# First block's query and key norm: mean squares with tokens on partitions, and one root and one reciprocal for all eight pairs

## What is computed

```python
h = rmsnorm(x, norm1_g[l])
proj = h @ w_in[l]
u, v_a, q, k, v_b = jnp.split(proj, splits, axis=-1)
...
q = rmsnorm(q.reshape(bsz, s, B_HEADS, 2, B_HEAD_DIM), q_norm_g[l]).transpose(0, 2, 3, 1, 4)
k = rmsnorm(k.reshape(bsz, s, B_HEADS, 2, B_HEAD_DIM), k_norm_g[l]).transpose(0, 2, 3, 1, 4)
```

## Time and profile before

| | us |
|---|---|
| median of 3 runs | 2310.82 |
| lowest and highest | 2306.65, 2314.41 |
| the profiled execution | 2307.06 |
| its span in the profile | 2305.3 |

### The profile page before, as it was taken

The page is one execution under the profiler, slowest core; times in us unless marked ns, Lnnn a source line. Parts: engine busy times, 40 slices in busy tenths (PEclk is TensorE's granted clock), DMA queues, the critical chain, the costliest instruction groups (busy, mean ns, idle before and its releaser), DMA issues.

```text
span 2305.3 us, 32023 instructions
## 1 busy us (share of the span) xinstructions
PE 2232.5 (97%) x13582; PEld 1820.1 (79%) x13582; DVE 1315.1 (57%) x1860; ACT 700.0 (30%) x966; POOL 206.1 (9%) x233
## 2 busy tenths in 40 slices
PE   7989988999999999999999999999999999999998
PEld 6778984555478888889679888888888888968998
DVE  5677544333377557543557755745756633656554
ACT  5445331111142122123453211223312212454333
POOL 2100200000011000030021100003000002002000
PEclk9999999999999999999999999999999999999999
DMA  9753756999956456432114545624636423405573
GB/s 296 250 207 116 250 206 250 420 421 421 404 172 192 136 156 184 124 116 69 49 38 128 173 144 166 184 89 122 183 117 202 147 86 106 128 20 144 160 203 117
DMA packets 377548, 408.86 MB, mean 177 GB/s; under 512 B 11625, under 2 KB 342878, under 8 KB 361150
## 3 DMA queue, kind: packets, MB, share of 16 engines
q1 hardware_dynamic: 355886, 325.55, 42.9%
q0 software_dynamic: 20928, 80.14, 10.5%
q10 hardware_dynamic: 592, 1.12, 0.1%
HBM read 405.71 MB, written 1.05 MB: 176 GB/s over the span
## 4 chain that ended last, share of the span: by engine, by line
PE 88%; DVE 7%; ACT 2%; DMA 1%; issue 1%; SPq 0%; POOL 0%; DVEq 0%; ACTq 0%
PE B L1815 23%; PE B L1817 22%; PE B L1816 22%; PE B L2210 6%; PE B L2230 3%; PE B L2181 2%; PE B L2169 2%; DVE LO L680 1%; PE B L2536 1%; DVE R L691 1%; DVE HF L1061 1%; PE B L2510 1%; ACT HI L1378 1%; PE B L1948 1%; PE B L2520 1%
## 5 line engine op out<-in xcount | busy, mean ns | idle before, releaser
L1815 PE MATMUL B<-hH,HI 128*128 128x512 f32 (+1 forms) x1936 | 661.6, 342 | 14.0 <-DVE hL L1049 6.5
L1816 PE MATMUL B<-hL,HI 128*128 128x512 f32 (+1 forms) x1936 | 653.5, 338 | 0.0
L1817 PE MATMUL B<-hH,LO 128*128 128x512 f32 (+1 forms) x1936 | 653.2, 337 | 0.0
L680 DVE TENSOR_TENSOR LO<-RAW,HI 128x2048 fp32r<-128x2048 f32 (+3 forms) x218 | 443.6, 2037 | 115.6 <-ACT HI L1378 109.8
L1378 ACT ACTIVATE HI<-RAW 128x2048 fp32r<-128x2048 f32 (+3 forms) x218 | 368.6, 1692 | 347.4 <-PE B L1817 274.0
L1815 PEld LDWEIGHTS B<-hH,HI 128*128 128x128 f32 x1936 | 368.2, 190 | 65.3 <-DVE LO L680 12.6
L1817 PEld LDWEIGHTS B<-hH,LO 128*128 128x128 f32 x1936 | 368.3, 190 | 39.7
L1816 PEld LDWEIGHTS B<-hL,HI 128*128 128x128 f32 x1936 | 368.6, 190 | 37.5 <-issue 0.2
L1815 PE MATMUL B<-aH,HI 128*128 128x512 f32 (+1 forms) x770 | 269.3, 350 | 0.4 <-DVE LO L680 0.4
L1817 PE MATMUL B<-aH,LO 128*128 128x512 f32 (+1 forms) x770 | 269.0, 349 | 0.0
L1816 PE MATMUL B<-aL,HI 128*128 128x512 f32 (+1 forms) x770 | 268.2, 348 | 0.0
(11 more groups left out here) (377 smaller groups left out, 2649.4 us busy)
## 6 DMA issues: line engine op xcount, KB each, us to landing
RAW<-in_ffn_w_gu SPq DMA_DIRECT2D x176, 512.0 KB, 5.2
W<-in_w SPq DMA_DIRECT2D x78, 1024.0 KB, 11.9
MADW<-in_ada_w POOLq DMA_DIRECT2D x112, 512.0 KB, 3.7
W2T<-in_w SPq DMA_DIRECT2D x39, 1024.0 KB, 12.1
RAW<-in_w_in SPq DMA_DIRECT2D x60, 512.0 KB, 5.1
RAW<-in_ffn_w_down SPq DMA_DIRECT2D x56, 384.0 KB, 3.7
RAW<-in_ffn_w_down SPq DMA_DIRECT2D x56, 320.0 KB, 4.3
RAW<-in_w_out SPq DMA_DIRECT2D x24, 512.0 KB, 4.4
```

Source lines behind the costliest of these rows:

```text
L680: V.tensor_tensor(LO[s][:, :words], RAW[s][:, :words], HI[t.hi[s]][:, :words].bitcast(F32), ALU.subtract).then_inc(lo_done[s], 1)
L1815: mm(o, wh, xh, start=first, stop=False, **more)
L1816: mm(o, wh, xl, start=False, stop=False, **more)
L1817: return mm(o, wl, xh, start=False, stop=last, **more)
```

## The change

For each pair, the four blocks of 128 features by 128 tokens of `SQ` now become the stationary operand, and two columns of `MEAN_HD` the moving one. The means come out with tokens on partitions, two columns for each block: 64 columns in B[2] for all eight pairs. After chunk 8, ACT takes one root of 128 x 64 and DVE one reciprocal of 128 x 64. PE then spreads the scales back to features with 64 products of a repeated column (64 columns wide) and the identity, four pairs after chunk 9 and four after chunk 10. DVE multiplies each pair with its gain and the scales straight from PSUM, four pairs in its step 10 and four in its step 11.

```diff
@@ names @@
+        FIRST_HEADS = (0, 4, 1, 5, 2, 6, 3, 7)
+        FIRST_BANKS = (0, 1, 3, 2)
+        FIRST_SCALES = 2 * TB * HEADS * 2
@@ VectorE @@
+            def scaled(n):
+
+                c = FIRST_HEADS[n]
+                got("spread_done")
+                gain = GQ[:, 0:1] if c < 4 else PT[:, KN:KN + 1]
+                V.scalar_tensor_tensor(pair(QK, c), pair(QK, c), gain, B[FIRST_BANKS[n % 4]][:], ALU.mult, ALU.mult)\
+                    .then_inc(E["qk_ready"], 1)
+
             for c in range(12):
                 prep()
                 t.use()
-                if 1 <= c <= 8:
-                    r = R[(c - 1) % 2][:]
-                    rstd(r)
-                    gain = GQ[:, 0:1] if c - 1 < 4 else PT[:, KN:KN + 1]
-                    V.scalar_tensor_tensor(pair(QK, c - 1), pair(QK, c - 1), gain, r, ALU.mult, ALU.mult)\
-                        .then_inc(E["qk_ready"], 1)
+                if c == 8:
+                    got("std_ready")
+                    r = R[0][:, 0:FIRST_SCALES]
+                    V.reciprocal(r, r).then_inc(E["qr_ready"], 1)
+                if c >= 9:
+                    for n in ((), range(0, 4), range(4, 8))[c - 9]:
+                        scaled(n)
@@ ScalarE @@
                     A.activation(pair(QK, c), B[4 + c % 2][:], ACT.Copy)
+                    if c >= 2:
+                        got("stats_done")
                     A.activation(SQ[c % 2][:], B[4 + c % 2][:], ACT.Square).then_inc(E["sq_ready"], 1)
...
-                if 1 <= c <= 8:
-                    if c >= 3:
-                        act.wait_ge(E["qk_ready"], c - 2)
-                    root(B[2 + (c - 1) % 2][:], R[(c - 1) % 2][:])
+                if c == 8:
+                    got("stats_done")
+                    root(B[2][:, 0:FIRST_SCALES], R[0][:, 0:FIRST_SCALES])
@@ TensorE @@
-            def stats(m, i, b, n=512):
-
-                claim(b, "std_ready")
-                got("sq_ready")
-                mm(B[b][:, :n], mat(m), SQ[i % 2][:, :n], start=True, stop=True).then_inc(E["stats_done"], 1)
-
+            def first_squares(i):
+
+                if i == 0:
+                    claim(2, "std_ready")
+                got("sq_ready")
+                for m in range(2):
+                    for blk in range(TB):
+                        c0 = 2 * (TB * (2 * i + m) + blk)
+                        ins = mm(B[2][:, c0:c0 + 2], SQ[i % 2][:, m * S + blk * P:m * S + (blk + 1) * P],
+                                 mat(MEAN_HD).rearrange("p (c n) -> p c n", c=2)[:, :, 0], start=True, stop=True)
+                ins.then_inc(E["stats_done"], 1)
+
+            def first_spread(n0):
+
+                for n in range(n0, n0 + 4):
+                    b = FIRST_BANKS[n % 4]
+                    claim(b, "qk_ready", n + 1)
+                    for m in range(2):
+                        for blk in range(TB):
+                            c0 = 2 * (TB * (2 * FIRST_HEADS[n] + m) + blk)
+                            for half in range(2):
+                                ins = mm(B[b][HD * half:HD * (half + 1), m * S + blk * P:m * S + (blk + 1) * P],
+                                         R[0][:, c0 + half:c0 + half + 1].to_broadcast([P, HD]), mat(IDENT),
+                                         start=True, stop=True)
+                    ins.then_inc(E["spread_done"], 1)
...
                 if 1 <= c <= 8:
-                    stats(MEAN_HD, c - 1, 2 + (c - 1) % 2)
+                    first_squares(c - 1)
+                elif c == 9:
+                    got("qr_ready")
+                    first_spread(0)
+                elif c == 10:
+                    first_spread(4)
```

## The result

| | us |
|---|---|
| before, median of 20 runs | 2311.34 (2305.44 to 2317.76) |
| changed, median of 20 runs | 2314.56 (2311.5 to 2318.15) |
| ratio, 95% interval | 1.0017 [1.001, 1.0024] |
| profiled execution of the changed kernel, its span | 2313.92, 2312.2 |

The changed kernel is 0.17% slower, 2.3 to 5.5 us by the interval: beyond chance, but under the 0.3% that the forecast took for a visible difference. The medians differ by 3.2 us. The forecast was +4 us.

A forecast was written before the change was run, and what follows sets the result against it. PE, busy 97% of the span, was taken as the bound, with DMA full after chunk 8. Terms -3.0 + 0.9 + 7.5 - 1.5 = +3.9, say +4 us on 2310.8, forecast 2315 us, range 2307 to 2322.

The forecast's parts named there:

- The late `LO`s: Chunks 2 to 8: PE's three waits for DVE's `LO` behind reciprocal and product go, -3.0 us.
- The means: PE in each pair's step: eight records of 0.109 us, 0.87 instead of 0.76 us a pair, +0.9 us in all.
- The spread: PE after chunks 9 and 10: 128 records at 0.057 us, 7.3, plus restarts, paid in full, +7.5 us.
- two restarts: PE at the spread's two groups: 0.1 us added for each, on top of 7.3 us of records.
- The wait in head 0: PE's 1.67 us wait for one `ada` unit's transfer goes; DVE can follow by at most 1.51, so -1.5 us.
- C: Stretch from 88 to 138 us is bound by transfers, which swallow the spread: -2 us, 2309, no change; chance 0.10.
- B: Spread's halves don't overlap, its products cost 13.9 instead of 7.3 us: +10.5 us, 2321, slower; chance 0.10.
- D: `LO` in chunks 2 to 8 and head 0's unit stay late: +8.5 us, 2319, slower; chance 0.08.
- E: Granted clock's short falls come or go at later places: 3 us either way on any case; upper end 0.06.
- F: More than the sum is won: kernel faster by over 7 us; chance 0.04.
- The hidden steps: After chunk 8, root and reciprocal, and DVE's products after chunks 9 and 10, finish before PE asks: no cost.
- stages far behind that differ by more than the shift: Sign at later stages: the prediction is wrong if they differ by more than the delay passed on.

The follow-up runs named there:

- e4: Kernel before with each reciprocal made in two halves of 256 columns, the second behind the next `LO`, no spread: ratio 0.9986, -3.2 us.
- e7: Changed kernel with each two-column product of the means made twice: one trace, chunk ends 7.54 us apart, 0.89 more.
- e1: Changed kernel with each spread product made twice: ratio 1.0042 to the kernel before, +9.7 us.
- e3: Kernel before with the spread's 64 products added after chunks 9 and 10, results unread: ratio 1.0013, +3.0 us.
- e2: Changed kernel with only a quarter of the spread's products: ratio 0.9981 to the kernel before, -4.4 us.
- e8: Kernel before with reciprocals of 64 instead of 512 columns and the spread's 64 products added after chunks 5 and 6: one trace, lag +3.75 us.
- e6: Kernel before, unchanged, executed once more for its trace: lag -0.30 us.

## Why the prediction was right, step by step

**The late `LO`s, -3.0.** Right in mechanism and in size. Chunks 2 to 8 lose no time any more; e4 wins 2.6 of the 3.0 us with DVE's order alone.

**The means, +0.9.** Right in sign, too large. The step in chunks 2 to 8 grew from 6.61 to 6.645, not to 6.72, and after chunk 8 it even shrank by 0.09 (91.55 - 82.97 = 8.58; before 94.14 - 85.47 = 8.67). The first pair's means add nothing: they fall into the wait of chunk 2, whose step is 7.78 us instead of 7.79. That is 0.2 - 0.1 = +0.1 in all, where +0.9 was forecast: the largest error of the sum. The row that it was taken from gives the price of the records right (e7), but eight records in this place cost less than eight times that.

**The spread, +7.5.** 3.66 and 3.65 us: 7.3. e1 and e3 show that each record is paid in full, and e1 rules out both other prices. The 0.2 for two restarts was counted on top of a price that has it already: the 3.65 us of the earlier trace rows hold 3.50 us of records (e1) and the fixed part, which is 0.16 to 0.17 us by e1 and e2.

The Trainium skill, TensorEngine Tiling (Array Packing), Key Properties, says that a change of tiling mode drains TensorE, and the prediction priced such a change at 0.16 us, an estimate. The traces agree with that size: 0.16 to 0.17 us with one change more (e1, e2), 0.33 with two (e8). The prediction's reading of 0.09 us from the entry alone was too small. That the time is a drain and nothing else that comes with the change, no run here shows.

**The wait in head 0, -1.5.** The chunk of head 0 ends 11.50 us after chunk 11, before 13.37: -1.9. The whole wait of 1.67 was won, and 0.2 of restart. I had held it to 1.5 by DVE's idle time; DVE had no share in it up to that point. That the spread takes the wait away is shown by e3. The time that the late unit has is the same with and without the spread: POOL begins to issue the two units of head 0 10.1 us before PE begins with the first of them (103.22 to 113.32 before, 107.93 to 118.04 in the changed kernel, and likewise in e2, e3, e4 and e8). So the unit landed sooner. My reason for that, releases further apart under full transfers, fits e3 and the changed kernel, where the DMA share is 0.80 (98 to 111 us) and 0.81 (95 to 106 us) ahead of this issue, and 1.05 before (94.5 to 103 us). It does not explain all: e4, e2 and e8 shorten the wait with little or no spread between the `ada` units and a share of 1.02 to 1.05. What does it there stays open.

**The sum.** -2.8 (late `LO`s and six means) - 0.1 + 7.3 - 1.9 = +2.5 against the +3.9 of the forecast: the trace's lag is +2.54. The times give 2.3 to 5.5. So 2.5 lies inside, at the lower end. That the forecast's 3.9 is also the ratio's middle is luck: the terms as they were measured give 1.4 less.

The rest of the measured time goes with the clock. The record has the mean granted clock of the 30 executions of the kernel before beside e1 to e4 and of the 20 of the changed one, though these were not run side by side. A straight line through both, with one slope, has 1.7 us for each 0.001 of mean clock, and puts the changed kernel 2.6 us behind at the same clock (1.6 to 3.7), beside the lag of 2.5; this is an estimate. In the same way e1, e2, e3 and e4 come out at +9.1, -2.2, +5.7 and -3.3, near the lags of their traces. The changed kernel's mean clock is 0.9874 against 0.9879, worth 1.0 us; that is not clear of the scatter between executions, so whether the change makes the clock fall more often is not shown.

**The rivals.** C fell with e1 and e3, B with the first trace and e1, D with the chunk ends. E was real: the single executions differ by 3 us and more through the clock, with no change of the program (e6), which goes with the 6.9 us between two traces where the medians differ by 3.2. F did not come. The hidden steps (root, reciprocal, DVE's products) were hidden: nothing on PE waits for them. One of the prediction's signs of being wrong did turn up, stages far behind that differ by more than the shift; e6 shows the same 3.6 us in the unchanged kernel.

## What to carry to other kernels

When an engine is late because of the order of its own work, change the order first: here two halves of a reciprocal around the urgent operation won 2.6 of the 3.0 us at no cost on PE, while moving the work to PE won the 3.0 and cost 7.4. An operation taken off an engine with idle time is worth only the waits that it caused; eight reciprocals were 26.8 us of DVE and 3.0 us of the kernel. And a product of two moving columns is not nearly free: a further record cost 0.11 us here (e7), the pace at which the loads of its 128-column weights stand in the trace (eight from 62.72 to 63.62). Turning the operands round didn't make the means cheaper.

## What the runs showed of the hardware that was not expected

The spread's products in two column halves cost 0.0546 us for each further record, beside 128-column or 32-column products, and each change of width that the spread added between products cost about 0.16 us once (e1, e2, e8). PE's granted clock in one stretch of 45 us was 0.96 in one execution and 0.89 in another of the same kernel, and its second execution was 3.6 us later by the end of it, as much as the whole effect under study. The comparison at equal clock, or of the trace up to the end of the changed stage, tells the two apart. A reciprocal took 0.55 us for 64 columns, 1.75 for 256 and 3.35 for 512: that is 0.15 us and 6.25 ns for each column, so splitting it in two costs 0.15 us.
